# Seven-product units in the feed-forward blocks of a decoder trunk: four a block instead of three, two low parts a block on GpSimd, another order of VectorE's sums

## The chip, the cores and the metric

The kernel runs on one core of a Trainium2 chip. The metric is the device time of one execution in microseconds (us). Engines are called by their names in the profile: PE is TensorE, DVE is VectorE, ACT is ScalarE, POOL is GpSimd, SP is SyncE, whose queue issues the loads of the weights.

## The reference, cut to what matters

The program is one layer of a hybrid decoder with 256 tokens, 2048 model columns and a feed-forward width of 5632. The change touches only its last part:

```
u = rmsnorm(h, pre_ffn_g)                                     # 256 x 2048
ff = (silu(u @ w_gate) * (u @ w_up)) @ w_down                 # 2048 -> 5632 -> 2048
h = h + rmsnorm(ff, post_ffn_g)
```

All inputs are float32.

## The kernel before

**Precision.** A float32 operand is split into a high part (rounded to the fp32r format of PE) and a low part (the rest). A product is then three matmuls into one PSUM bank: high by high, high by low, low by high (`three`, L1705). ACT makes the high parts of the weights (`split_hi`, L557, line L561 in the profile), DVE the low parts as `raw - w_hi` (`split_lo`, L908, line L910).

**Stages.** After the mixing layers (up to 346 us) come eleven feed-forward blocks, g = 0 to 10 (`NFG`). A block makes 512 columns of gate and 512 of up. Its 16 chunks q = BEGIN[g] + ch (ch = 0 to 15) each hold 128 rows of w_gate and w_up side by side, 128x1024 float32, 512 KB, loaded with two DMAs (line L447). Two blocks of w_down with 44 chunks each follow (g = 11 and 12). Everything goes through a ring of four slots (`WSLOTS`): `raw` (loaded), `w_hi`, `w_lo`. Chunk q + 4 takes the slot of chunk q.

**Plain chunks and seven-product units.** A plain chunk is four quarters (two halves of the tokens, gate and up) of three matmuls each: 12 matmuls of 128x512. Two successive chunks can also form a *unit of seven products* (Strassen-Winograd): 7 products instead of 8, so 21 matmuls instead of 24. `ROUND` says by a letter for each pair of chunks whether it is plain (P) or a unit (Z); before, blocks 1 to 10 have `PPZPZPZP`, that is units at ch 4-5, 8-9 and 12-13. A unit needs sums of the weights, which DVE makes in `weight_sums` (L1186): sum 0 (L1197, 128x512), the low half of the first chunk (L1183), sum 1 (L1202), and sums 2 and 3 in one instruction (L1206, 128x1024). Then comes the low part of the second chunk (L910), and after ACT's high parts of the sums (L841, two of 128x1024), their low parts (`weight_sums_lo`, L1213, two of 128x1024). Sum 0 waits for the raw data of both chunks. The sums stand in one buffer, `tx`. A unit also needs sums of the token rows (`input_sums`, made once for each pair of row tiles in `SEVEN_F`, in block 0).

**The end of a block.** When PE has done a block's last unit, ACT copies one PSUM bank to `tx` (`x0_kept`, L891), in its program behind the high part of ch 1 of the next block, and DVE makes `fold_sums` (L1267, L1271, L1274), in its program behind the low part of ch 1. When PE has done the whole block, DVE adds them to the quarters (`fold`, L1280 twice, and `fold_up`, L1284), ACT takes the silu (L818), DVE multiplies (`gated`, L1171 twice): this is `inner_product`, at ch 3 of the next block. PE then transposes the result (`turn_inner`, L1769) ahead of ch 2, for which it waits for `p_done`, the end of the second L1171. ACT and DVE split the transposed tiles (`inner_hi`, L822; `inner_lo`, L1176, semaphore `f_lo`), at ch 5 (`INNER_AT`).

**Banks.** PE transposes into two banks that the products m7 and m6 of the block's units use. So in the block's first unit PE waits ahead of m6 for `inner_lo`:

```
three(m5, row_sum(0), weight_sum(0), begin, end).then_inc(t_used, 1)
if begin and g <= NFG:
    pe.wait_ge(f_lo, g)
three(m6, row_sum(1), weight_sum(1), begin, end).then_inc(t_used, 1)
```

**Order and slots.** Each engine runs its program in the order of q, as written out in the loops over q; nothing is reordered. SP issues the loads in the order of q. For the load of chunk q it waits until chunk q - 4 has its low part (`lo_done`), and, if q - 4 is in a unit, until that unit's sums 2 and 3 are made:

```
if (before, d_b) in SEVEN_NO:
    sp_eng.wait_ge(t_made, 3 * SEVEN_NO[before, d_b] + 3)
```

ACT makes the high part of chunk q once it is loaded and PE has used chunk q - 4 (`chunks_used`). POOL's program ends before the feed-forward blocks begin.

Of the kernel before, what the change touches and what calls it, by code (L numbers as in the profile page):

```python
# [24 lines left out]
P = 128  # L25
# [11 lines left out]
def build_trunk(nc, x, meta, pre_mix_g, w_in, w_pool, pool_scale, w_dw, b_dw, conv_ln_g, conv_ln_b, w_pw,  # L37
# [93 lines left out]
    ROUND = ["PPPPPPPP"] + ["PPZPZPZP"] * (NFG - 1) + ["PPPPZPPZPPZPPZPZPZPZPP", "PPPZPZPZPZPZPZPZPZPZPP"]  # L131
    BEGIN = [Q_FFN + KT * g for g in range(NFG)] + [Q_DOWN + FT * n for n in range(DW)]
# [12 lines left out]
    QUARTERS = [(0, 0), (0, 1), (1, 0), (1, 1)]  # L145
    INNER_AT = 5
    FOLDS_F = len(QUARTERS) * (NFG - 1)
    assert DW == 2 and ROUND[NG - 1].endswith("P" * (LAST // 2)) and all(d in SUM_NO for d in SEVEN_U)

    def place_of(q):  # L150
        g = max(g for g in range(NG) if BEGIN[g] <= q)
        ch = q - BEGIN[g]
        return g, ch, TURNS[g][ch // 2]

    def landed(q):
# [5 lines left out]
    with ExitStack() as ctx:  # L161
# [37 lines left out]
        sums_f = sb_at("sums_f", [P, len(SEVEN_F), 4, 2, P], F32R, a_y)  # L199
        gated = sb_at("gated", [P, NQ, DCOLS], F32, a_y + 4 * KT * SEQ - 8 * DCOLS)  # L200
        sums_y = sb_at("sums_y", [P, max(len(SEVEN_U) - IN_U, 1), 3, 2, P], F32R, a_y)
        assert 32 * P * len(SEVEN_F) + 8 * DCOLS <= 4 * KT * SEQ and 24 * P * (len(SEVEN_U) - IN_U) <= 4 * KT * SEQ
# [108 lines left out]
        def sem(name):  # L311
            return ctx.enter_context(nc.semaphore(name))
# [87 lines left out]
        def _(sp_eng):  # L400
# [64 lines left out]
        def _(pool):  # L465
# [90 lines left out]
        def _(act):  # L556
# [350 lines left out]
        def _(dve):  # L907
# [278 lines left out]
            def weight_sums(q, z):  # L1186

                at = [(q - 1) % WSLOTS, q % WSLOTS]
                b11, b12, b22 = (raw[:, at[k], j * DCOLS:(j + 1) * DCOLS] for k, j in ((0, 0), (0, 1), (1, 1)))
                for k in range(2):  # L1190
                    dve.wait_ge(raw_landed[at[k]], landed(q - 1 + k))
                if z == 0:
                    dve.wait_ge(s_lo, 2 * len(SEVEN_F))
                else:
                    dve.wait_ge(t_used, 4 * z - 3)
                    dve.wait_ge(fold_done, len(QUARTERS) * max(min(SEVENS[z][0], NFG) - 1, 0))
                dve.tensor_tensor(tx[:, 0, :], b12, b11, ALU.add).then_inc(t_made, 1)  # L1197
# [169 lines left out]
        def _(pe):  # L1367
# [346 lines left out]
            def right(q, j):  # L1714
                at = slice(j * DCOLS, (j + 1) * DCOLS)
                return [w_hi[:, q % WSLOTS, at], w_lo[:, q % WSLOTS, at]]

            def plain_products(q, quarters):
                g, ch, d = place_of(q)
                kt, chs = 2 * d + ch % 2, 2 * len(ROUND[g])  # L1720
                pe.wait_ge(lo_done, q + 1)
                if g >= NFG:
                    pe.wait_ge(f_lo, kt // 4 + 1)
                for m, j in quarters:
                    if g == 0:
                        pe.wait_ge(h2_lo, CK * m + kt + 1 if kt < CK else CK + kt + 1)
                    mm = three(quarter(g, m, j), left(g, kt, m), right(q, j), ch == 0, ch == chs - 1)
                return mm

            def seven_products(q):  # L1730
# [110 lines left out]
```

## Time and profile before

| | |
|---|---|
| median of 3 runs | 1076.29 us (1075.73 to 1076.4) |
| the profiled execution, its own time | 1075.67 us |
| its span in the profile | 1073.7 us |
| PE busy | 1063.8 us (99%), 5731 matmuls |
| DVE busy | 891.5 us (83%) |
| ACT busy | 598.3 us (56%) |
| POOL busy | 31.5 us (3%) |
| granted clock of PE | 0.999 of full speed |
| DMA, mean | 194 GB/s |

The own time is the span and some 2 us around it. In the rows below a time is in us from the start of the span. In a timeline a row is: start, duration, engine, line, operation, output and inputs, shape, how many were merged, and in brackets the idle time before it with what ended it. Instructions of one engine overlap a little: the next one starts before the one ahead of it ends. So what an instruction occupies on its engine is the distance from its start to the next start, not its duration.

### The profile page before, as it was taken

Reading aid. Unit: us, or ns where it says so; the run is one execution under the profiler, and the core shown is the slowest. Engines: PE = TensorE matmul, PEld = TensorE weight load, DVE = VectorE, ACT = ScalarE, POOL = GpSimd, SP = SyncE. Lnnn points to the kernel's source line nnn. Section 1 sums busy time; section 2 is a strip of 40 time slices with the busy share of each in tenths; the row PEclk is TensorE's granted clock in tenths of the full one; section 3 lists DMA queues with packets and bytes.
Section 4 is the critical chain, followed back from the end, with each engine's and each line's share of the span. In section 5 each row is a group of like instructions: output and inputs, shape, how many; then the busy total and the mean of one; then the engine's idle time right before and its main releaser. Section 6 shows DMA issues by size and latency. Waiting matters only on the chain. (4 is left out here: it accounts for less than half of the span.)

```text
span 1073.7 us, 15358 instructions
## 1 busy us (share of the span) xinstructions
PE 1063.8 (99%) x5731; PEld 921.6 (86%) x5731; DVE 891.5 (83%) x1082; ACT 598.3 (56%) x735; POOL 31.5 (3%) x49
## 2 busy tenths in 40 slices
PE   9999999999999999999999999999999999999997
PEld 8999999999888888888888888888888888888885
DVE  6699987646646787898998998988989899988887
ACT  6554454736545565555565655655655555655553
POOL 6000001101000000000000000000000000000000
PEclk9999999999999999999999999999999999999999
DMA  8655535444386475756756656657656666566665
GB/s 271 216 176 166 172 105 162 135 143 135 112 309 214 140 266 185 225 188 193 223 174 195 216 180 212 195 181 231 189 185 222 223 200 197 189 208 214 208 200 196
DMA packets 113208, 208.06 MB, mean 194 GB/s; under 512 B 9184, under 2 KB 46496, under 8 KB 111856
## 3 DMA queue, kind: packets, MB, share of 16 engines
q1 hardware_dynamic: 111952, 201.49, 58.8%
q10 hardware_dynamic: 608, 4.20, 1.0%
q0 software_dynamic: 576, 1.40, 0.4%
q8 instruction: 46, 0.75, 0.3%
q14 instruction: 26, 0.21, 0.1%
HBM read 202.86 MB, written 4.19 MB: 193 GB/s over the span
## 5 line engine op out<-in xcount | busy, mean ns | idle before, releaser
L561 ACT ACTIVATE w_hi<-raw 128x1024 fp32r<-128x1024 f32 x321 | 337.1, 1059 | 259.0 <-PE ps L1708 153.0
L910 DVE TENSOR_TENSOR w_lo<-raw,w_hi 128x1024 fp32r<-128x1024 f32 x321 | 389.6, 1226 | 84.0 <-ACT w_hi L561 83.4
L1706 PE MATMUL ps<-w_hi,uf 128*128 128x512 f32 x524 | 205.3, 392 | 0.1
L1708 PE MATMUL ps<-w_hi,uf 128*128 128x512 f32 x524 | 204.1, 389 | 0.0
L1707 PE MATMUL ps<-w_lo,uf 128*128 128x512 f32 x524 | 203.9, 389 | 0.0
L1377 PE MATMUL ps<-u,w_hi 128*128 128x272 f32 (+1 forms) x544 | 158.8, 292 | 0.0
L1379 PE MATMUL ps<-u,w_hi 128*128 128x272 f32 (+1 forms) x544 | 155.9, 287 | 0.0
L1380 PE MATMUL ps<-u,w_lo 128*128 128x272 f32 (+1 forms) x544 | 155.7, 286 | 0.0
L841 ACT CAST t_hi<-tx 128x1024 fp32r<-128x1024 f32 x92 | 96.4, 1053 | 67.7 <-DVE tx L1202 56.4
L1708 PEld LDWEIGHTS ps<-w_hi,uf 128*128 128x128 f32 x524 | 98.4, 188 | 20.6
L1706 PEld LDWEIGHTS ps<-w_hi,uf 128*128 128x128 f32 x524 | 98.4, 188 | 20.5 <-issue 0.5
L1707 PEld LDWEIGHTS ps<-w_lo,uf 128*128 128x128 f32 x524 | 98.4, 188 | 20.0
L1213 DVE TENSOR_TENSOR t_lo<-tx,t_hi 128x1024 fp32r<-128x1024 f32 x92 | 108.2, 1218 | 0.0
L1377 PEld LDWEIGHTS ps<-u,w_hi 128*128 128x128 f32 x544 | 102.4, 188 | 0.4
L1379 PEld LDWEIGHTS ps<-u,w_hi 128*128 128x128 f32 x544 | 102.5, 188 | 0.2
L1380 PEld LDWEIGHTS ps<-u,w_lo 128*128 128x128 f32 x544 | 102.5, 188 | 0.0
L1706 PE MATMUL ps<-w_hi,ffn 128*128 128x512 f32 x256 | 99.7, 389 | 0.0
L1708 PE MATMUL ps<-w_hi,ffn 128*128 128x512 f32 x256 | 99.6, 389 | 0.0
L1707 PE MATMUL ps<-w_lo,ffn 128*128 128x512 f32 x256 | 99.6, 389 | 0.0
L1206 DVE TENSOR_TENSOR tx<-raw,tx 128x1024 f32<-128x1024 f32 x46 | 56.4, 1226 | 4.7
L1707 PEld LDWEIGHTS ps<-w_lo,ffn 128*128 128x128 f32 x256 | 48.1, 188 | 10.0
L1708 PEld LDWEIGHTS ps<-w_hi,ffn 128*128 128x128 f32 x256 | 48.1, 188 | 9.9
(277 smaller groups left out, 1473.2 us busy)
## 6 DMA issues: line engine op xcount, KB each, us to landing
raw<-in_w_gate SPq DMA_DIRECT2D x176, 256.0 KB, 3.0
raw<-in_w_up SPq DMA_DIRECT2D x176, 256.0 KB, 3.5
raw<-in_w_down SPq DMA_DIRECT2D x88, 512.0 KB, 4.2
raw<-in_w_in SPq DMA_DIRECT2D x72, 512.0 KB, 3.6
raw<-in_w_out SPq DMA_DIRECT2D x32, 512.0 KB, 4.7
arena<-in_x SPq DMA_DIRECT2D x2, 1024.0 KB, 6.2
arena<-in_x ACTq DMA_DIRECT2D x2, 1024.0 KB, 8.7
out<-h2rows SPq DMA_DIRECT2D x2, 1024.0 KB, 5.5
```

The source lines that it names most:

```text
L561: act.activation(w_hi[:, slot, :], raw[:, slot, :], ACT.Copy).then_inc(hi_done, 1)
L841: act.copy(t_hi[:, 2 * h:2 * h + 2, :], tx[:, 2 * h:2 * h + 2, :]).then_inc(t_hi_done, 1)
L910: dve.tensor_tensor(w_lo[:, slot, :], raw[:, slot, :], hi_view(w_hi[:, slot, :]), ALU.subtract).then_inc(lo_done, 1)
L1206: dve.tensor_tensor(tx[:, 2:4, :], raw[:, at[0]:at[0] + 2, 0:DCOLS], tx[:, 1:2, :].to_broadcast([P, 2, DCOLS]), ALU.add).then_inc(t_made, 1)
L1213: dve.tensor_tensor(t_lo[:, 2 * h:2 * h + 2, :], tx[:, 2 * h:2 * h + 2, :], hi_view(t_hi[:, 2 * h:2 * h + 2, :]), ALU.subtract).then_inc(t ...
L1377: pe.matmul(outs[m], w_hi[:, slot, at], x_hi, start=start and not (one_bank and m), stop=False, skip_group_check=True)
L1379: pe.matmul(outs[m], w_hi[:, slot, at], x_lo, start=False, stop=False, skip_group_check=True)
L1380: mm = pe.matmul(outs[m], w_lo[:, slot, at], x_hi, start=False, stop=last and k == len(kts) - 1, skip_group_check=True)
L1706: pe.matmul(o, a[0], b[0], start=start, stop=False)
L1707: pe.matmul(o, a[0], b[1], start=False, stop=False)
L1708: return pe.matmul(o, a[1], b[0], start=False, stop=stop)
```

## The change

It does four things. Blocks 1 to 7 (`WITH_SPARE`) get a fourth unit: `PZPZPZZP`, units at ch 2-3, 6-7, 10-11 and 12-13; blocks 8 to 10 keep their order. In those blocks `inner_hi` and `inner_lo` stand at ch 4, and the first unit's sums (ch 3) stand in DVE's program ahead of `inner_product`, its low parts behind it; ACT makes the high parts of that unit's sums ahead of the high part of ch 3. POOL makes two of DVE's low parts a block: of ch 3 of blocks 1 to 7 (`IN_PRODUCT`, after the first `fold`) and of ch 1 of blocks 2 to 8 (`IN_FOLD`, after ACT's copy of x0); PE and SP wait for these on a semaphore of their own, `lo_pool`. The sums get a second buffer (`tx2`, `t_hi2`, `t_lo2`), which the units of blocks 1 to 7 use in turn. And in every unit, those of the later blocks too, the low part of the second chunk (`split(q)`) moves up between sum 1 and sums 2 and 3. Block 0 makes the row sums of a fourth pair.

```diff
-    SEVEN_F, SEVEN_U = (0, 1, 2), (11, 12, 13, 14, 15, 16, 17, 18, 19)
+    SEVEN_F, SEVEN_U = (0, 1, 2, 3), (11, 12, 13, 14, 15, 16, 17, 18, 19)
-    F_SUM_AT = {10: 0, 12: 1, 14: 2}
-    ROUND = ["PPPPPPPP"] + ["PPZPZPZP"] * (NFG - 1) + [...]
+    F_SUM_AT = {10: 0, 12: 1, 13: 2, 14: 3}
+    WITH_SPARE = range(1, 8)
+    ROUND = ["PPPPPPPP"] + ["PZPZPZZP" if g in WITH_SPARE else "PPZPZPZP" for g in range(1, NFG)] + [...]
-    INNER_AT = 5
+    INNER_AT = [4 if g in WITH_SPARE else 5 for g in range(NFG + 1)]
+    IN_PRODUCT = {BEGIN[g] + 3: g for g in WITH_SPARE}
+    IN_FOLD = {BEGIN[g + 1] + 1: g for g in WITH_SPARE}
+    BY_POOL = sorted([*IN_PRODUCT, *IN_FOLD])
...
+    def buffers_of(z):
+        g, d = SEVENS[z]
+        return (z - SEVENS_TO[g - 1] + 1) % 2 if g in WITH_SPARE else 0
...
@@ SP
-                sp_eng.wait_ge(lo_done, q - WSLOTS + 1)
+                if q - WSLOTS in POOL_NO:
+                    sp_eng.wait_ge(lo_pool, POOL_NO[q - WSLOTS] + 1)
+                else:
+                    sp_eng.wait_ge(lo_done, lo_by_dve(q - WSLOTS))
@@ POOL
+            for q in BY_POOL:
+                slot = q % WSLOTS
+                if q in IN_FOLD:
+                    pool.wait_ge(x0_kept, IN_FOLD[q])
+                elif IN_PRODUCT[q] > 1:
+                    pool.wait_ge(fold_done, len(QUARTERS) * (IN_PRODUCT[q] - 2) + 1)
+                pool.wait_ge(hi_done, q + 1)
+                pool.tensor_tensor(w_lo[:, slot, :], raw[:, slot, :], w_hi[:, slot, :].bitcast(F32),
+                                   ALU.subtract).then_inc(lo_pool, 1)
@@ ACT
                     if z is not None and ch % 2 == 0:
                         first_half_hi(q)
+                    elif q in IN_PRODUCT:
+                        weight_sums_hi(z)
+                        split(q)
                     else:
                         split(q)
@@ DVE, weight_sums
                 dve.tensor_tensor(sums[:, 1, :], b22, sums[:, 0, :], ALU.subtract).then_inc(t_made, 1)
+                if q not in POOL_NO:
+                    split(q)
...
                 dve.tensor_tensor(sums[:, 2:4, :], ...).then_inc(t_made, 1)
@@ DVE, loop over q
+                    if q in IN_PRODUCT:
+                        weight_sums(q, z)
                     if 1 <= g <= NFG and ch == 3:
                         dve.wait_ge(chunks_used, BEGIN[g])
                         inner_product(g - 1)
-                    if z is None:
+                    if z is None and q not in POOL_NO:
                         split(q)
-                    elif ch % 2:
+                    elif q in IN_PRODUCT:
+                        weight_sums_lo(z)
+                    elif z is not None and ch % 2:
                         weight_sums(q, z)
-                        split(q)
                         weight_sums_lo(z)
-                    if 1 <= g <= NFG and ch == INNER_AT:
+                    if 1 <= g <= NFG and ch == INNER_AT[g]:
                         inner_lo(g - 1)
```

## Rows read from the trace of the kernel before

**Rows 1.** The page: busy time, share of the span and instructions of each engine.
```profile
PE 1063.8 (99%) x5731; PEld 921.6 (86%) x5731; DVE 891.5 (83%) x1082; ACT 598.3 (56%) x735; POOL 31.5 (3%) x49
```
**Rows 2.** Busy time of each engine in one block (stretch; length, then engines; clock, DMA).
```profile
454.70:497.10 42.40, 42.40 (x193) 35.18 (x192) 38.59 (x40) 24.11 (x27) 0.00 (x0) 1.00 0.64 198
```
**Rows 3.** Timeline of PE: chunks 0 and 1 of block 3, transposes, chunk 2.
```profile
497.06 0.39 PE L1707 MATMUL ps<-w_lo,uf 128*128 128x512 f32 x1
...
502.04 0.39 PE L1708 MATMUL ps<-w_hi,uf 128*128 128x512 f32 x1
502.28 1.03 PE L1769 MATMUL ps<-cst,gated 128*128 128x128 f32 x8
503.07 0.48 PE L1706 MATMUL ps<-w_hi,uf 128*128 128x512 f32 x1
```
**Rows 4.** Timeline of DVE: a unit (ch 12-13 of block 2) and its low parts.
```profile
479.52 0.69 DVE L1197 TENSOR_TENSOR tx<-raw 128x512 f32<-128x512 f32 x1 [0.51 <-PE ps L1708]
480.12 0.68 DVE L1183 TENSOR_TENSOR w_lo<-raw,w_hi 128x512 fp32r<-128x512 f32 x1
480.73 0.68 DVE L1202 TENSOR_TENSOR tx<-raw,tx 128x512 f32<-128x512 f32 x1
481.51 1.23 DVE L1206 TENSOR_TENSOR tx<-raw,tx 128x1024 f32<-128x1024 f32 x1
482.66 1.22 DVE L910 TENSOR_TENSOR w_lo<-raw,w_hi 128x1024 fp32r<-128x1024 f32 x1
483.79 2.35 DVE L1213 TENSOR_TENSOR t_lo<-tx,t_hi 128x1024 fp32r<-128x1024 f32 x2
486.06 1.22 DVE L910 TENSOR_TENSOR w_lo<-raw,w_hi 128x1024 fp32r<-128x1024 f32 x1
```
**Rows 5.** Timeline of DVE: fold sums and inner product between blocks 2 and 3.
```profile
492.28 0.69 DVE L1267 TENSOR_TENSOR tx<-ps,tx 128x512 f32<-128x512 f32 x1 [0.80 <-ACT tx L891]
...
494.33 0.69 DVE L1274 TENSOR_TENSOR tx<-ps,tx 128x512 f32<-128x512 f32 x1
...
497.13 1.30 DVE L1280 TENSOR_TENSOR ps<-ps,tx 128x512 f32<-128x512 f32 x2 [0.44 <-PE ps L1708]
...
499.76 1.41 DVE L1171 SCALAR_TENSOR_TENSOR gated<-ps,cst,gated 128x512 f32<-128x512 f32 x2 [0.20 <-DVE ps L1284]
501.08 1.22 DVE L910 TENSOR_TENSOR w_lo<-raw,w_hi 128x1024 fp32r<-128x1024 f32 x1
```
**Rows 6.** Timeline of ACT: copy of x0 for that fold.
```profile
491.59 0.59 ACT L891 COPY tx<-ps 128x512 f32<-128x512 f32 x1 [1.60 <-PE ps L1708]
```
**Rows 7.** Timelines of POOL, DVE in the mixing stage: POOL alone, then both at once.
```profile
189.87 1.27 POOL L533 TENSOR_TENSOR side<-side 128x512 f32<-128x512 f32 x1 [21.52 <-ACT side L726]
...
248.62 1.99 POOL L533 TENSOR_TENSOR side<-side 128x512 f32<-128x512 f32 x1 [55.80 <-ACT side L741]
...
249.51 2.18 DVE L910 TENSOR_TENSOR w_lo<-raw,w_hi 128x1024 fp32r<-128x1024 f32 x1
251.62 0.47 DVE L975 SCALAR_TENSOR_TENSOR ffn<-ps,cst,ffn 128x256 fp32r<-128x256 f32 x1
...
250.69 1.60 POOL L535 TENSOR_TENSOR side<-side 128x256 f32<-128x256 f32 x1
```
**Rows 8.** Timelines of DVE, SP, ACT: sums made, four DMAs, wait for them.
```profile
504.21 1.23 DVE L1206 TENSOR_TENSOR tx<-raw,tx 128x1024 f32<-128x1024 f32 x1
...
506.97 0.43 SPq L447 DMA_DIRECT2D raw<-in_w_up  x1
...
511.23 1.06 ACT L561 ACTIVATE w_hi<-raw 128x1024 fp32r<-128x1024 f32 x1 [0.80 <-DMA raw<-in_w_up]
```
**Rows 9.** Timeline of ACT at the start of block 1: high part, table load, silu.
```profile
412.31 1.06 ACT L561 ACTIVATE w_hi<-raw 128x1024 fp32r<-128x1024 f32 x1 [1.66 <-PE ps L1708]
413.39 1.28 ACT L818 ACT_TABLE_LOAD   x1
414.68 1.27 ACT L818 ACTIVATE gated<-ps,cst 128x512 f32<-128x512 f32 x2
```

More of the change, by code:

```diff
@@ L126, in build_trunk @@
     NG = NFG + DW
-    SEVEN_F, SEVEN_U = (0, 1, 2), (11, 12, 13, 14, 15, 16, 17, 18, 19)
+    SEVEN_F, SEVEN_U = (0, 1, 2, 3), (11, 12, 13, 14, 15, 16, 17, 18, 19)
     SUM_AT = {4: 11, 10: 12, 12: 13, 18: 14, 22: 15, 24: 16, 28: 17, 32: 18, 36: 19}
     SUM_NO = {d: i for i, d in enumerate(SUM_AT.values())}
-    F_SUM_AT = {10: 0, 12: 1, 14: 2}
-    ROUND = ["PPPPPPPP"] + ["PPZPZPZP"] * (NFG - 1) + ["PPPPZPPZPPZPPZPZPZPZPP", "PPPZPZPZPZPZPZPZPZPZPP"]
+    F_SUM_AT = {10: 0, 12: 1, 13: 2, 14: 3}
+    WITH_SPARE = range(1, 8)
+    ROUND = ["PPPPPPPP"] + ["PZPZPZZP" if g in WITH_SPARE else "PPZPZPZP" for g in range(1, NFG)] + ["PPPPZPPZPPZPPZPZPZPZPP", "PPPZPZPZPZPZPZPZPZPZPP"]
     BEGIN = [Q_FFN + KT * g for g in range(NFG)] + [Q_DOWN + FT * n for n in range(DW)]
@@ L153, in place_of, with lo_by_dve, before_in_buffers @@
         return g, ch, TURNS[g][ch // 2]
+    IN_PRODUCT = {BEGIN[g] + 3: g for g in WITH_SPARE}
+    IN_FOLD = {BEGIN[g + 1] + 1: g for g in WITH_SPARE}
+    BY_POOL = sorted([*IN_PRODUCT, *IN_FOLD])
+    POOL_NO = {q: i for i, q in enumerate(BY_POOL)}
+    def lo_by_dve(q):
+        return q + 1 - sum(1 for a in BY_POOL if a <= q)
+    def buffers_of(z):
+        g, d = SEVENS[z]
+        return (z - SEVENS_TO[g - 1] + 1) % 2 if g in WITH_SPARE else 0
+    def before_in_buffers(z):
+        return max((y for y in range(z) if buffers_of(y) == buffers_of(z)), default=None)
     def landed(q):
@@ L192, in build_trunk @@
         t_hi = sb_at("t_hi", [P, 4, DCOLS], F32R, a_xt + 16 * DCOLS)
+        a_spare = top[0] + 4 * KT * SEQ + 4 * 1152 + 4 * 4 * (max(WITH_SPARE) + 1) * 2 * SEQ
+        tx2 = sb_at("tx2", [P, 4, DCOLS], F32, a_spare)
+        t_lo2 = sb_at("t_lo2", [P, 4, DCOLS], F32R, a_spare)
+        t_hi2 = sb_at("t_hi2", [P, 4, DCOLS], F32R, a_spare + 16 * DCOLS)
+        sums_of, hi_of, lo_of = (tx, tx2), (t_hi, t_hi2), (t_lo, t_lo2)
         rows_u = tx[:, 0, :].rearrange("p (k t) -> p k t", k=2)
@@ L199, in build_trunk @@
         sums_f = sb_at("sums_f", [P, len(SEVEN_F), 4, 2, P], F32R, a_y)
-        gated = sb_at("gated", [P, NQ, DCOLS], F32, a_y + 4 * KT * SEQ - 8 * DCOLS)
+        gated = sb_at("gated", [P, NQ, DCOLS], F32, a_spare + 32 * DCOLS)
         sums_y = sb_at("sums_y", [P, max(len(SEVEN_U) - IN_U, 1), 3, 2, P], F32R, a_y)
-        assert 32 * P * len(SEVEN_F) + 8 * DCOLS <= 4 * KT * SEQ and 24 * P * (len(SEVEN_U) - IN_U) <= 4 * KT * SEQ
+        assert 32 * P * len(SEVEN_F) <= 4 * KT * SEQ and 24 * P * (len(SEVEN_U) - IN_U) <= 4 * KT * SEQ
         side = sb_at("side", [P, KT * SEQ], F32, a_y)
@@ L207, in build_trunk @@
         a_ff = place(4 * FT * 2 * SEQ)
+        assert a_spare == a_ff + 4 * 32 * 2 * SEQ and 32 * DCOLS + 8 * DCOLS <= 4 * 12 * 2 * SEQ
         ffn = sb_at("ffn", [P, FT, 2, SEQ], F32R, a_ff)
@@ L1191, in weight_sums @@
                     dve.wait_ge(raw_landed[at[k]], landed(q - 1 + k))
-                if z == 0:
+                sums, y = sums_of[buffers_of(z)], before_in_buffers(z)
+                if z <= 1:
                     dve.wait_ge(s_lo, 2 * len(SEVEN_F))
-                else:
-                    dve.wait_ge(t_used, 4 * z - 3)
+                if y is not None:
+                    dve.wait_ge(t_used, 4 * y + 1)
+                if y is not None and buffers_of(z) == 0:
                     dve.wait_ge(fold_done, len(QUARTERS) * max(min(SEVENS[z][0], NFG) - 1, 0))
-                dve.tensor_tensor(tx[:, 0, :], b12, b11, ALU.add).then_inc(t_made, 1)
+                dve.tensor_tensor(sums[:, 0, :], b12, b11, ALU.add).then_inc(t_made, 1)
                 first_half_lo(q - 1)
-                if z:
-                    dve.wait_ge(t_used, 4 * z - 2)
+                if y is not None:
+                    dve.wait_ge(t_used, 4 * y + 2)
                 dve.wait_ge(t_made, 3 * z + 1)
-                dve.tensor_tensor(tx[:, 1, :], b22, tx[:, 0, :], ALU.subtract).then_inc(t_made, 1)
-                if z:
-                    dve.wait_ge(t_used, 4 * z)
+                dve.tensor_tensor(sums[:, 1, :], b22, sums[:, 0, :], ALU.subtract).then_inc(t_made, 1)
+                if q not in POOL_NO:
+                    split(q)
+                if y is not None:
+                    dve.wait_ge(t_used, 4 * y + 4)
                 dve.wait_ge(t_made, 3 * z + 2)
-                dve.tensor_tensor(tx[:, 2:4, :], raw[:, at[0]:at[0] + 2, 0:DCOLS],
-                                  tx[:, 1:2, :].to_broadcast([P, 2, DCOLS]), ALU.add).then_inc(t_made, 1)
+                dve.tensor_tensor(sums[:, 2:4, :], raw[:, at[0]:at[0] + 2, 0:DCOLS],
+                                  sums[:, 1:2, :].to_broadcast([P, 2, DCOLS]), ALU.add).then_inc(t_made, 1)
             def weight_sums_lo(z):
+                b = buffers_of(z)
                 dve.wait_ge(t_made, 3 * z + 3)
@@ L1212, in weight_sums_lo @@
                     dve.wait_ge(t_hi_done, 2 * z + h + 1)
-                    dve.tensor_tensor(t_lo[:, 2 * h:2 * h + 2, :], tx[:, 2 * h:2 * h + 2, :],
-                                      hi_view(t_hi[:, 2 * h:2 * h + 2, :]), ALU.subtract).then_inc(t_lo_done, 1)
+                    dve.tensor_tensor(lo_of[b][:, 2 * h:2 * h + 2, :], sums_of[b][:, 2 * h:2 * h + 2, :],
+                                      hi_view(hi_of[b][:, 2 * h:2 * h + 2, :]), ALU.subtract).then_inc(t_lo_done, 1)
             def four_sums(i, hi, lo, r, s):
@@ L1303, in _ @@
                         inner_product(g - 1)
-                    if z is None:
+                    if z is None and q not in POOL_NO:
                         split(q)
-                    elif ch % 2:
+                    elif q in IN_PRODUCT:
+                        weight_sums_lo(z)
+                    elif z is not None and ch % 2:
                         weight_sums(q, z)
-                        split(q)
                         weight_sums_lo(z)
-                    if 1 <= g <= NFG and ch == INNER_AT:
+                    if 1 <= g <= NFG and ch == INNER_AT[g]:
                         inner_lo(g - 1)
@@ L1716, in right, with weights_split @@
                 return [w_hi[:, q % WSLOTS, at], w_lo[:, q % WSLOTS, at]]
+            def weights_split(q):
+                if q in POOL_NO:
+                    pe.wait_ge(lo_pool, POOL_NO[q] + 1)
+                else:
+                    pe.wait_ge(lo_done, lo_by_dve(q))
             def plain_products(q, quarters):
@@ L1720, in plain_products @@
                 kt, chs = 2 * d + ch % 2, 2 * len(ROUND[g])
-                pe.wait_ge(lo_done, q + 1)
+                weights_split(q)
                 if g >= NFG:
@@ L1740, in weight_sum @@
                 def weight_sum(t):
-                    return [t_hi[:, t, :], t_lo[:, t, :]]
-                pe.wait_ge(lo_done, q + 1)
+                    return [hi_of[buffers_of(z)][:, t, :], lo_of[buffers_of(z)][:, t, :]]
+                weights_split(q)
                 if g < NFG:
```

6 lines of the change are left out of this document (4 added, 2 removed).

## The prediction

> **What bounds the kernel now.** The page's first part: PE is busy for 1063.8 us, 99% of the span [rows 1]. The busy time by stretches says how that is inside a block: a feed-forward block of three units takes 42.40 us, in which PE never rests and DVE is busy for 38.59 us, ACT for 24.11 [rows 2]. So fewer matmuls shorten the kernel, if their operands come in time. PE's timeline gives prices: 22 matmuls from 497.06 to 502.04, 0.226 us each; transposes to next chunk 0.8 us [rows 3].
>
> **T** below is the moment at which PE is done with a block; DVE's fold, which waited for it, started at 497.13, so T = 497.1 [rows 5]. PE started its transposes at T + 5.2 and chunk 2 at T + 6.0 [rows 3]: it needs `p_done` by T + 5.2.
>
> **The gain.** Seven units more, one in each of blocks 1 to 7, save three matmuls each: 21 x 0.226 = 4.8 us. A block would take 42.4 - 0.7 = 41.7 us. If nothing else moved, that would be the result. I think it does not get there, for two reasons.
>
> **Prices on DVE**, as distances between starts [rows 4]: a 128x512 sum or half low part 0.60; a low part, or sums 2 and 3, 1.14; `t_lo` of a unit 2.27 (483.79 to 486.06). Sums 2 and 3 right behind sum 1 start 0.78 after it, as they wait for its result. `fold_sums` takes 2.66 (492.28 to 494.33 and 0.61), `inner_product` 3.95 (497.13 to 501.08) [rows 5]. A unit with its second low part takes 3 x 0.60 + 2 x 1.14 + 2.27 = 6.4; its sums 2 and 3 are made 4.2 after its first sum starts (0.6 + 0.6 + 0.6 + 1.14 + 1.23), where they were before it 3.2: the move of the low part fills a gap of 0.1 us and makes the sums 1 us later, and SP's loads into the unit's two slots wait for the sums.
>
> DVE's work in a block of four units: three units 19.2; the first unit, whose second low part is POOL's, 0.6 + 0.6 + 0.78 + 1.14 = 3.1 for the sums and 2.27 for `t_lo`; seven of the eight plain chunks' low parts 8.0; `fold_sums`, `inner_product`, `inner_lo` 2.66 + 3.95 + 1.14. Together 40.3 of the 41.7 us. DVE can afford 1.4 us of waits a block; now it has 42.4 - 38.6 = 3.8 [rows 2].
>
> **A low part on POOL.** POOL alone took 1.27 us for 512 elements [rows 7], and 0.6 for 256 (the 1.60 of its row, 250.69 to 252.29, less the 1.0 in which DVE's operation, until 251.69, still held it up). Stretched to 1024 that is 2.4 (four times 0.6) to 2.6 (1.27 and two steps of 0.67); I take 2.4, as each of the short ones has its start in it, and 0.14 until it starts, an estimate. The rows also show who stands still: POOL's 1.99 ends at 250.61, DVE's low part, both inputs in SBUF, started at 249.51 and took 2.18 in place of 1.22, to 1.08 after POOL's end; but DVE's L975, which reads PSUM and one SBUF tensor, took 0.47 in the middle of a POOL operation [rows 7]. So POOL's low part of ch 1 is free beside `fold_sums`, and that of ch 3 beside the folds, but not beside `t_lo`.
> By the Trainium skill ("GPSIMD Engine Reference", Performance versus the Vector engine) GpSimd's add of 2048 float32 elements takes 4497 ns, so an estimate of 2.25 us for 1024. With it the loop below would be 0.15 us shorter and the result some 1 us lower; no run yet shows that size.
>
> **First reason: the bank of m6.** ACT copies x0 at T - 5.5 [rows 6], once PE is done with the last unit; DVE starts `fold_sums` at T - 4.8 [rows 5]. It is done at T - 2.2, and the new first unit's sums 3.1 later. Call **W** the moment at which DVE is free of them: W = T + 1.0 at the earliest. From there: `inner_product` 4.05 (ACT's silu now stands behind two high parts, of the sums and of ch 3, and is just in time: W + 0.1 + 2 x 1.0, first silu to W + 2.7, gated after it), so `p_done` at W + 4.15 = T + 5.15, met by a hair. POOL's low part of ch 3 starts when its high part is made, W + 2.15 + 0.14, and ends at W + 4.7: DVE's first `t_lo` waits 0.6 for it. Then 2.27, low part of ch 4 1.14, `inner_lo` 1.22: W + 9.3 = T + 10.3. PE, though, now has its first unit at ch 2: it starts at T + 6.0, and after 12 matmuls, at T + 8.7, waits for `inner_lo` to give back the bank of m6. It stands still 1.6 us, 1.0 even if POOL holds nobody up. Before, the first unit was at ch 4, 5.4 us later. So even with DVE on time the block takes 41.7 + 1.0 to 1.6, **more than the 42.4 of before**.
>
> **Second reason: DVE's loop through the loads.** After sums 2 and 3 of a unit (end 505.44) SP issues two chunks, and ACT starts on the second at 511.23: 5.8 us [rows 8]. The next unit's sum 0 waits for both. In the new order:
> 1. W to sums 2, 3 of unit 2 (ch 6-7): 4.05 + 0.6 + 2.27 + 1.14 + 1.14 + 1.14 + 4.2 = 14.5.
> 2. Unit 3 (ch 10-11) takes unit 2's slots: 5.8 + 4.2 = 10.0. DVE has only `t_lo` and two low parts in between (4.5), so it waits 1.3.
> 3. Unit 4 (ch 12-13) right after: 2.2 + 4.2 = 6.4.
> 4. Ch 0 and 1 of the next block take unit 4's slots: 5.8 to ch 1's data, 1.06 for its high part [rows 8], 0.6 for x0 behind it [rows 6]: 7.5 to `fold_sums`. DVE waits 1.8.
> 5. `fold_sums` and the next first sums: 2.66 + 3.14 = 5.8.
> Sum 44.2 us from W to W, where PE would need 41.7. So DVE falls behind, and from block 3 on every block takes 44.2: PE waits for `p_done` and `inner_lo`.
> The same steps for the order of before (three units four chunks apart, two low parts in between) give under 40: there PE leads, as the trace shows.
>
> **The sum.** Block 1: DVE's program in block 0 is 2.3 us longer (the fourth row sums), hidden from PE. T is 412.3, when ACT could begin the high part of ch 3, and I estimate W = 413.6, much as in the later blocks. ACT's high parts of sums 2 and 3 and of ch 3 come ahead of its one table load (1.28) and the silu (1.27) [rows 9]: 415.7, 417.0, 418.3, and the second gated ends at 419.1, where PE wants it at 417.5: 1.6 lost; the bank costs 0.9 more. T of block 2 is 454.7 - 0.7 + 2.5 = 456.5. Its W, by steps 2 to 5, is 458.5; five loops on, W of block 7 is 458.5 + 5 x 44.2 = 679.5; and PE from W: chunk 2 at W + 5.0, 14 chunks of 156 matmuls 35.7 with the gap at their start, bank 1.6, gives W + 42.3 = 721.8 for the end of block 7. Before it is 497.1 + 5 x 42.4 = 709.1. Loss **12.7**. Blocks 8 to 10 and w_down have the old order: DVE catches up in block 8 behind `fold_sums`, and the low part moved there costs nothing, since DVE waits for PE in every unit there (0.5 before sum 0 [rows 4]); without that cover it would be 1 us a unit. The last stretch is unchanged. The profiled execution's 1075.7 (span 1073.7 and 2.0 around it), 0.6 under the median, would become 1088.4; the median 1076.3 becomes **1089.0**.
> Bounds: if the loop is 43.4 (data 0.4 sooner each time, POOL in nobody's way) the loss is 8.7; if it is 45.0 (POOL's 2.6, loads 0.3 later) 16.7.
>
> **Rivals.**
> *A, the loads do not bind* (they land sooner, or DVE is ahead): then only the bank holds PE, 0.3 to 0.9 a block more than before, six times, and 1.8 in block 1: 4 to 7 us, 1076.3 + 5.4 = 1081.7. For: DVE's work alone fits (40.3). Against: 5.8 us for the second load. 15%.
> *B, faster*: `inner_lo` is done before PE gets to m6, and the loads do not bind. It decides at T + 8.7: `inner_lo` would have to be done 1.6 us sooner than I find. Then the saved 21 matmuls count in full: 1076.3 - 4.8 = 1071.5. Against: the four steps on DVE ahead of it, all priced. 10%.
> *C, POOL stops all of DVE*, PSUM operations too: 2.4 more in `fold_sums` and 1 in `inner_product`, six times: 20 us more, 1109. Against: L975's 0.47 beside POOL [rows 7]. The Trainium skill ("SBUF — State Buffer", Who interferes with whom) also has DVE instructions with one SBUF input free of GpSimd; by it the sum stays. 4%.
> *D, gain and wait cancel*: the bank alone, and a wait of only 0.7 a block: 1076.3. 4%.
>
> **Chances.** Main case 67%, its own range 1085 to 1093 by the bounds. The range of 8 in 10 takes in most of A: 1079 to 1093. A measurement of this kernel can tell some 0.2% (2 us) from no change. Faster by over 0.2%: 0.10 (B); within: 0.05 (D, the edge of A); slower: 0.85.
>
> **What would show it.** Right: PE idle in each of blocks 2 to 7, some 1.6 us ahead of the first L1706 of m6, released by DVE's L1176, and some ahead of L1769, released by L1171; DVE idle 1.3 before sum 0 of unit 3 (released by a load) and 1.8 before L1267; blocks of 44.2 us; POOL's 14 low parts at 2.4 to 2.6; `t_lo` once a block at 1.8 in place of 1.22. Wrong: PE without gaps and blocks of 41.7 (B); gaps only at m6 and blocks of 43 (A); L1267 and L1271 longer beside POOL (C).

## The result, and the profile after

| | before | after |
|---|---|---|
| median of the runs | 1076.01 us (4 runs, 1075.68 to 1076.4) | 1090.95 us (4 runs, 1089.71 to 1091.37) |
| ratio, 95% interval | | 1.0137 (1.0124 to 1.0149) |
| span in the profile | 1073.7 us | 1089.5 us |

The change makes the kernel 1.4% slower; predicted were 1089.0 us, in a range of 1079 to 1093. The first part of the page after answers to [rows 1]:

```profile
PE 1061.8 (97%) x5710; PEld 914.7 (84%) x5710; DVE 908.5 (83%) x1109; ACT 605.7 (56%) x750; POOL 65.1 (6%) x63
```

PE has the 21 matmuls less that were forecast (5731 to 5710), POOL 14 instructions more. PE is no longer busy all the time (97% of the span in place of 99%). The list of waits of the profile after, 400 to 745 us (who waited for whom: us in total, times, longest):

```profile
ACT w_hi L599 <- DMA raw<-in_w_up: 27.9, 28, 2.8
...
DVE tx L1314 <- ACT tx L933: 12.3, 7, 3.2
...
PE ps L1825 <- DVE gated L1213: 8.3, 7, 1.8
PE ps L1756 <- DVE ffn L1218: 7.5, 7, 1.2
```

The last two are the waits of the prediction: seven ahead of the transposes (L1825, released by `gated`) and seven ahead of m6 (L1756, released by `inner_lo`). Before there was none of either. L1314 is the first instruction of `fold_sums`, which waits for x0. Its starts give the length of the blocks, and this is how blocks are measured in all that follows: the distance from the first to the seventh of these instructions, by six. After:

```profile
453.65 0.69 DVE L1314 TENSOR_TENSOR tx<-ps,tx 128x512 f32<-128x512 f32 x1 [1.17 <-ACT tx L933]
...
676.40 0.69 DVE L1314 TENSOR_TENSOR tx<-ps,tx 128x512 f32<-128x512 f32 x1 [1.46 <-ACT tx L933]
```

The seventh stands at 720.38: (720.38 - 453.65) / 6 = 44.5 us, where before it was (704.21 - 449.87) / 6 = 42.4. Behind the seventh start the distances are 42.2, 41.8 and 42.4, about those of before. DVE's timeline of the kernel after, where block 3 begins (the counterpart of [rows 5]):

```profile
497.95 0.69 DVE L1314 TENSOR_TENSOR tx<-ps,tx 128x512 f32<-128x512 f32 x1 [1.68 <-ACT tx L933]
498.74 1.23 DVE L1318 TENSOR_TENSOR tx<-ps,tx 128x1024 f32<-128x1024 f32 x1
500.00 0.69 DVE L1321 TENSOR_TENSOR tx<-ps,tx 128x512 f32<-128x512 f32 x1
500.82 0.70 DVE L1241 TENSOR_TENSOR tx<-raw 128x512 f32<-128x512 f32 x1
...
502.82 1.23 DVE L1252 TENSOR_TENSOR tx<-raw,tx 128x1024 f32<-128x1024 f32 x1
503.96 1.29 DVE L1327 TENSOR_TENSOR ps<-ps,tx 128x512 f32<-128x512 f32 x2
...
508.02 2.80 DVE L1260 TENSOR_TENSOR t_lo<-tx,t_hi 128x1024 fp32r<-128x1024 f32 x2
...
511.88 1.21 DVE L1218 TENSOR_TENSOR ffn<-ps,ffn 128x1024 fp32r<-128x1024 f32 x1
```

POOL's timeline in the same stretch:

```profile
497.92 2.41 POOL L582 TENSOR_TENSOR w_lo<-raw,w_hi 128x1024 fp32r<-128x1024 f32 x1 [33.83 <-ACT tx L933]
506.24 2.37 POOL L582 TENSOR_TENSOR w_lo<-raw,w_hi 128x1024 fp32r<-128x1024 f32 x1 [5.91 <-ACT w_hi L599]
```

And PE's, the counterpart of [rows 3]:

```profile
508.16 1.09 PE L1825 MATMUL ps<-cst,gated 128*128 128x128 f32 x8 [1.15 <-DVE gated L1213]
...
511.63 0.39 PE L1758 MATMUL ps<-t_hi,sums_f 128*128 128x512 f32 x1
513.15 0.50 PE L1756 MATMUL ps<-t_hi,sums_f 128*128 128x512 f32 x1 [1.13 <-DVE ffn L1218]
513.48 0.40 PE L1757 MATMUL ps<-t_lo,sums_f 128*128 128x512 f32 x1
```

In these three the reader sees: POOL's first low part (497.92 to 500.33) lies beside `fold_sums`, which takes what it took before; its second (506.24 to 508.61) meets `t_lo`, whose pair takes 2.80 in place of 2.35. `inner_lo` ends at 513.09, and PE, which could have gone on at 511.9, starts m6 at 513.15.

### The profile page after: what moved, and what is told of

Read it like the earlier page. It is cut to its first block and busy times, and to the rows that moved or that the text cites. A ratio compares the mean times of both kernels' runs of the same rounds, so it can differ in the third digit from the quotient of the medians.

```text
span 1089.5 us, 15429 instructions
## 1 busy us (share of the span) xinstructions
PE 1061.8 (97%) x5710; PEld 914.7 (84%) x5710; DVE 908.5 (83%) x1109; ACT 605.7 (56%) x750; POOL 65.1 (6%) x63
## 5 line engine op out<-in xcount | busy, mean ns | idle before, releaser
L599 ACT ACTIVATE w_hi<-raw 128x1024 fp32r<-128x1024 f32 x314 | 328.3, 1058 | 199.6 <-PE ps L1758 65.1
L952 DVE TENSOR_TENSOR w_lo<-raw,w_hi 128x1024 fp32r<-128x1024 f32 x300 | 364.6, 1226 | 77.6 <-ACT w_hi L599 76.8
L1756 PE MATMUL ps<-w_hi,uf 128*128 128x512 f32 x482 | 189.0, 392 | 0.5 <-DVE tx L1321 0.4
L1758 PE MATMUL ps<-w_hi,uf 128*128 128x512 f32 x482 | 187.7, 389 | 0.0
L1757 PE MATMUL ps<-w_lo,uf 128*128 128x512 f32 x482 | 187.6, 389 | 0.0
L880 ACT CAST t_hi<-tx 128x1024 fp32r<-128x1024 f32 x106 | 111.7, 1053 | 130.9 <-DVE tx L1246 71.8
L1260 DVE TENSOR_TENSOR t_lo<-tx,t_hi 128x1024 fp32r<-128x1024 f32 x106 | 127.7, 1246 | 1.6
L1756 PEld LDWEIGHTS ps<-w_hi,uf 128*128 128x128 f32 x482 | 90.5, 188 | 19.7 <-DVE tx L1321 0.8
L1758 PEld LDWEIGHTS ps<-w_hi,uf 128*128 128x128 f32 x482 | 90.5, 188 | 18.9
L1757 PEld LDWEIGHTS ps<-w_lo,uf 128*128 128x128 f32 x482 | 90.5, 188 | 18.3
L1756 PE MATMUL ps<-w_hi,ffn 128*128 128x512 f32 x256 | 99.7, 389 | 0.0
L1252 DVE TENSOR_TENSOR tx<-raw,tx 128x1024 f32<-128x1024 f32 x53 | 64.5, 1218 | 0.7
L582 POOL TENSOR_TENSOR w_lo<-raw,w_hi 128x1024 fp32r<-128x1024 f32 x14 | 33.5, 2392 | 436.5 <-ACT tx L933 238.7
L1756 PEld LDWEIGHTS ps<-w_hi,ffn 128*128 128x128 f32 x256 | 48.0, 188 | 10.0
## 6 DMA issues: line engine op xcount, KB each, us to landing
arena<-in_x ACTq DMA_DIRECT2D x2, 1024.0 KB, 10.2
```

The source lines that it names most:

```text
L582: pool.tensor_tensor(w_lo[:, slot, :], raw[:, slot, :], w_hi[:, slot, :].bitcast(F32), ALU.subtract).then_inc(lo_pool, 1)
L599: act.activation(w_hi[:, slot, :], raw[:, slot, :], ACT.Copy).then_inc(hi_done, 1)
L880: act.copy(hi_of[b][:, 2 * h:2 * h + 2, :], sums_of[b][:, 2 * h:2 * h + 2, :]).then_inc(t_hi_done, 1)
L952: dve.tensor_tensor(w_lo[:, slot, :], raw[:, slot, :], hi_view(w_hi[:, slot, :]), ALU.subtract).then_inc(lo_done, 1)
L1252: dve.tensor_tensor(sums[:, 2:4, :], raw[:, at[0]:at[0] + 2, 0:DCOLS], sums[:, 1:2, :].to_broadcast([P, 2, DCOLS]), ALU.add).then_inc(t_ma ...
L1260: dve.tensor_tensor(lo_of[b][:, 2 * h:2 * h + 2, :], sums_of[b][:, 2 * h:2 * h + 2, :], hi_view(hi_of[b][:, 2 * h:2 * h + 2, :]), ALU.subt ...
```

## The experiments

Theory L: two things hold PE. The first is a loop, DVE's work and the loads that wait for a unit's sums; it sets the length of a block. The second is the bank of m6, which would set it if the loop were shorter. Against L stand a theory that counts the bank alone (K), and smaller ones named with each run. A result outside the range that was expected is called a miss. "Blocks" is the measure above; the kernel before has 42.4, the kernel after 44.5. Times are medians beside the kernel before on the same chip (1076.1 in the first four, 1075.7 to 1075.8 in the others).

**e1_order_alone.** Kernel before, with one move:
```diff
                 dve.tensor_tensor(tx[:, 1, :], b22, tx[:, 0, :], ALU.subtract).then_inc(t_made, 1)
+                split(q)
...
                         weight_sums(q, z)
-                        split(q)
                         weight_sums_lo(z)
```


> The kernel before, with only the new place of a unit's second low part (between sum 1 and sums 2 and 3), in all units. Theory L (after the change it is DVE's loop through the loads that sets the length of a block): three units stand four chunks apart, so the sums 1 us later stay hidden behind PE's lead; time as before, 1075 to 1077, TensorE without gaps. Rival M (the moved low part is costly by itself, in every unit and in w_down too): 46 units at up to 1 us, 1080 or more.

Measured: 1076.39 us, ratio 1.0002 (0.9992 to 1.0012). No difference that these runs can tell, and PE waits for nothing from 400 to 745 us. The move costs nothing where PE leads.

**e2_low_part_back.** Kernel after, the same move undone in every unit.
```diff
-                if q not in POOL_NO:
-                    split(q)
...
                                   sums[:, 1:2, :].to_broadcast([P, 2, DCOLS]), ALU.add).then_inc(t_made, 1)
+                if q not in POOL_NO:
+                    split(q)
```


> The kernel after, with the second low part back behind sums 2 and 3 in every unit; the rest stays. Theory L: the sums of units 2 and 3 are ready 1 us sooner each, so the loop shrinks from the measured 44.4 us to about 42.5, less than TensorE needs with its wait for the bank (41.7 + 1.6 = 43.3): blocks of 43.3, 1083 us (1081 to 1086), the waits for L1213 (turning) mostly gone, those for L1218 (bank of m6) as they are. Rival K (only the bank counts, and the wait ahead of the transposes follows from it): no change, 1090.

Measured: 1084.25 us, ratio 1.0077 (1.0061 to 1.0094); blocks 43.3. 6.7 us of the 15 come from a move that cost nothing in e1. The waits of this kernel, 400 to 745 us:
```profile
PE ps L1756 <- DVE ffn L1218: 7.7, 7, 1.2
...
PE ps L1825 <- DVE gated L1213: 1.8, 1, 1.8
```
Ahead of the transposes only block 1's wait is left; the bank is as before. So the block is now what PE needs with its wait for the bank. ACT says the same: its copy of x0, which in the kernel after starts right behind the high part of ch 1 in all seven blocks, now waits for PE:
```profile
579.97 1.06 ACT L599 ACTIVATE w_hi<-raw 128x1024 fp32r<-128x1024 f32 x1 [1.15 <-DMA raw<-in_w_up]
581.48 0.59 ACT L933 COPY tx<-ps 128x512 f32<-128x512 f32 x1 [0.45 <-PE ps L1758]
```
Rival K, which wanted 1090, falls.

**e3_x0_first.** Kernel after, ACT's x0 ahead of the high part of ch 1 (and no longer behind it).
```diff
+                    if q in IN_FOLD:
+                        act.wait_ge(t_used, 4 * SEVENS_TO[g - 1])
+                        act.copy(tx[:, 0, :], sevens_bank(g - 1, 0)).then_inc(x0_kept, 1)
                     if z is not None and ch % 2 == 0:
                         first_half_hi(q)
```


> The kernel after, with ACT's copy of x0 ahead of the high part of ch 1 in place of behind it (blocks 2 to 8), so that the fold sums no longer wait for a load. Theory L: the loop shrinks by the 1.7 us and more that DVE waits there (measured 1.2 to 3.2), to 42.5 or so; TensorE's wait for the bank then sets the block: 43.3, 1083 us (1081 to 1086). Rival K: no change, 1090.

Measured: 1089.29 us, ratio 1.0122 (1.0105 to 1.0139); blocks 44.3. A miss: 1083 was expected. DVE's timeline of this run shows why:
```profile
540.95 0.69 DVE L1317 TENSOR_TENSOR tx<-ps,tx 128x512 f32<-128x512 f32 x1 [0.86 <-ACT tx L905]
541.74 1.23 DVE L1321 TENSOR_TENSOR tx<-ps,tx 128x1024 f32<-128x1024 f32 x1
543.00 0.69 DVE L1324 TENSOR_TENSOR tx<-ps,tx 128x512 f32<-128x512 f32 x1
544.62 1.03 DVE L1244 TENSOR_TENSOR tx<-raw 128x512 f32<-128x512 f32 x1 [0.92 <-DMA raw<-in_w_up]
```
The fold sums wait less (0.86 where the kernel after waits 3.21 in that block, its longest; 3.9 in place of 12.3 us in all), but right behind them sum 0 waits 0.92 for a load, and then runs 1.03 beside POOL. Behind the wait that was taken away lay another (the load), and behind that POOL's hold. The theory becomes L2: once unit 4's sums are made, the loads of chunks 0 to 3 follow each other, and the last sets when the next unit's sum 0 can start.

**e4_bank_late.** Kernel after, the bank freed in time: `inner_hi`, `inner_lo` at the end of ch 3, and in a block's first unit
```diff
+                if begin and g in WITH_SPARE:
+                    pe.wait_ge(t_lo_done, 2 * z + 2)
+                    three(quarter(g, 1, 0), left(g, 2 * d + 1, 1), weight_sum(3)).then_inc(t_used, 1)
                 if begin and g <= NFG:
                     pe.wait_ge(f_lo, g)
```
(the units of these blocks then wait for all four products of the unit whose buffer they take).

> The kernel after, with the wait for the bank of m6 taken away: in blocks 1 to 7 DVE's inner_lo and ACT's inner_hi stand at the end of ch 3, ahead of the low and high part of ch 4, and TensorE does the product for quarter (1,0) of a block's first unit ahead of m6. Theory L: the seven waits for L1218 (8.6 us in all) go, but the wait ahead of the transposes grows by as much, since DVE's loop keeps its 44.4 us: 1088 to 1091. Rival K: the 8.6 us are won, 1082.

Measured: 1089.2 us, ratio 1.0126 (1.0109 to 1.0143); blocks 44.2. Its waits, 400 to 745 us:
```profile
PE ps L1832 <- DVE gated L1213: 10.3, 7, 1.7
PE ps L1756 <- DVE tx L1321: 3.2, 6, 0.9
```
The seven waits for the bank (7.5 us) are gone. The wait ahead of the transposes has grown from 8.3 to 10.3, and the one in the second row from 0.4 to 3.2: PE, early in a block, waits for the last of the fold sums (L1321). Of the 7.5 us, 4.8 came back in these two, and the time fell by 1.8. With the loop in place, the bank was nearly free. DVE has a new wait in this run, 8.1 us ahead of sum 0 (8 times, put down to nothing that the profile shows). The last load of a pair landed 0.08 us before each of these starts (in block 3 it was issued at 519.50 and landed 4.2 us later, and sum 0 of unit 3 starts at 523.77), so it is the loads that DVE waits for, and not the four products.

**e5_loads_lighter.** e3, with fewer bytes in the row of loads: of the up half of chunks 2 and 3 only 64 of 512 columns are loaded, so part of the up projection is left out.
```diff
+                        n = 64 if j and ch in (2, 3) and g in IN_FOLD.values() else DCOLS
-                        sp_eng.dma_start(raw[:, q % WSLOTS, j * DCOLS:(j + 1) * DCOLS],
+                        sp_eng.dma_start(raw[:, q % WSLOTS, j * DCOLS:j * DCOLS + n],
```


> The kernel of e3_x0_first, in which the fold sums came sooner but sum 0 of a block's first unit then waited 0.8 to 0.9 us for loads. Here the up half of chunks 2 and 3 of blocks 1 to 7 is loaded for 64 of its 512 columns (the rest of it is what the slot held, so that this part of the up projection is left out); everything else is issued as before. Theory L2 (four chunks are loaded in a row once unit 4's sums are made, and their bytes set when sum 0 can start): 0.45 MB less in the row of four makes it land some 1.8 us sooner, the wait of L1244 for a load goes, blocks shrink by 0.8 us or more toward the 43.3 that TensorE needs with its bank: 1084 (1082 to 1086). Rival N (the wait has to do with the place in the program or in the queue, not with bytes): 1089 as e3.

Measured: 1086.96 us, ratio 1.0105 (1.0088 to 1.0122); blocks 43.8. The same place in DVE's timeline:
```profile
541.49 0.69 DVE L1325 TENSOR_TENSOR tx<-ps,tx 128x512 f32<-128x512 f32 x1
542.10 1.29 DVE L1245 TENSOR_TENSOR tx<-raw 128x512 f32<-128x512 f32 x1
```
The wait for the load is gone with the bytes, so L2 holds and rival N falls. But the time is 1 us above the range, a miss. More than half of what the 0.9 us could bring is lost at once: sum 0, started sooner, meets POOL's low part (540.44 to 542.85) and takes 1.29 in place of 0.69.

**e6_no_pool.** Kernel after, `BY_POOL` empty, ch 3's low part ahead of `t_lo` on DVE.

> The kernel after, with VectorE making the two low parts again (that of ch 3 ahead of the first unit's low parts, that of ch 1 ahead of the fold sums). Theory L: ch 1's part falls into VectorE's wait ahead of the fold sums and costs nothing; ch 3's costs its 1.14 us less the 0.45 that GpSimd held t_lo up (2.80 in place of 2.35): blocks 0.7 us longer, 1095 (1093 to 1098). Rival P (GpSimd holds VectorE up by as much as it takes off it): 1090 or less.

Measured: 1105.92 us, ratio 1.0276 (1.0256 to 1.0296); blocks 46.5. A miss by 11 us, and rival P is further off. DVE at the turn from one block to the next:
```profile
547.78 1.23 DVE L952 TENSOR_TENSOR w_lo<-raw,w_hi 128x1024 fp32r<-128x1024 f32 x1 [2.03 <-ACT w_hi L599]
548.93 0.68 DVE L1314 TENSOR_TENSOR tx<-ps,tx 128x512 f32<-128x512 f32 x1
```
The expectation put ch 1's low part into DVE's wait ahead of the fold sums. But it has to wait for the same high part as x0, and stands behind that wait: 1.15 in place of x0's 0.65. That and ch 3's 0.7 make 1.2 of the 2.0 us a block. The rest lies between the sums of unit 2 and those of unit 4 (17.5 us on the mean of the six blocks, in place of 16.5). In four of the six blocks DVE waits there ahead of ch 9's low part for ACT, and ACT for PE:
```profile
575.14 1.23 DVE L952 TENSOR_TENSOR w_lo<-raw,w_hi 128x1024 fp32r<-128x1024 f32 x1 [1.49 <-ACT w_hi L599]
```
```profile
574.05 1.06 ACT L599 ACTIVATE w_hi<-raw 128x1024 fp32r<-128x1024 f32 x1 [1.66 <-PE ps L1759]
```
So a late PE can hold the loop up in turn; what makes it late there was not tried. POOL's two low parts are worth 15 us against DVE making them at these places: they are the good half of the change.

**e7_bank_and_low_part** is e2 and e4 together.

> e2 and e4 together: second low part back behind the sums, and the bank of m6 freed in time. Each alone left the other limit. Theory L: the loop is then 13.4 + 9.0 + 6.5 + 7.5 + 5.8 = 42.2 us, TensorE's own need 41.7: blocks of 42.2, and block 1's wait for its silu stays (2.0 less 0.7): 1076 to 1079. Rival Q (the low part and the bank act on the same wait, so that together they bring no more than the better one): 1084.

Measured: 1079.98 us, ratio 1.0039 (1.0025 to 1.0054), 1 us above the range, a miss. e2 alone won 6.7 us and e4 alone 1.8, together they win 11.0: two limits one behind the other, so rival Q falls. (The profiled execution took 1083.34, so its blocks, 43.2, are longer than the median's.)

**e8_all_four** is e7 with e3, and with POOL's start in ch 3 brought forward:
```diff
                     elif q in IN_PRODUCT:
-                        weight_sums_hi(z)
+                        weight_sums_hi(z, [0])
                         split(q)
+                        weight_sums_hi(z, [1])
```


> e7_bank_and_low_part with x0 copied ahead of ch 1's high part, and ACT's high part of ch 3 between the two halves of the unit's high sums, so that GpSimd's part of ch 3 starts 1 us sooner and is done when t_lo begins. Theory L: the loop falls under TensorE's 41.7 us or just to it, the transposes are met by a hair: blocks of 41.7 to 42, 1073.5 (1072 to 1077). Rival L2 (the row of four loads keeps the loop where it is): as e7_bank_and_low_part.

Measured: 1077.44 us, the median of ten runs, one of which took 5216.82; without that one it is 1077.09, and the ratio 1.0012 (1.0002 to 1.0022) is taken from the nine. Blocks 42.6. Just above the range, a miss, though 3 us better than e7, which rival L2 had put it level with. DVE's timeline:
```profile
582.63 0.69 DVE L1245 TENSOR_TENSOR tx<-raw 128x512 f32<-128x512 f32 x1 [0.91 <-DMA raw<-in_w_up]
...
589.72 2.35 DVE L1264 TENSOR_TENSOR t_lo<-tx,t_hi 128x1024 fp32r<-128x1024 f32 x2
```
`t_lo` is back at 2.35, as meant. Sum 0 waits 0.91 for the row of loads.

**e9_own_chunk.** e8; sum 0 reads only the unit's first chunk, so it waits for that one alone.
```diff
-                for k in range(2):
-                    dve.wait_ge(raw_landed[at[k]], landed(q - 1 + k))
+                dve.wait_ge(raw_landed[at[0]], landed(q - 1))
...
+                dve.wait_ge(raw_landed[at[1]], landed(q))
                 dve.wait_ge(t_made, 3 * z + 1)
```


> e8_all_four, and a unit's sum 0 waits for its first chunk's data alone (it reads no other); the wait for the second chunk's data stands ahead of sum 1, 1.2 us later, in all units. Theory L2: what is left in e8 is VectorE's wait of 0.9 us for chunk 3's load behind the fold sums, which comes out as TensorE's 0.7 us ahead of the transposes in six blocks; it goes, blocks come to 41.8: 1073.5 (1072.5 to 1075), under the kernel before. Rival R (the 0.7 us come from ACT's chain up to the silu): no change, 1077.

Measured: 1075.55 us, ratio 0.9998 (0.9989 to 1.0007); blocks 42.3. A miss, half of what was expected: 1.5 to 1.9 us less than e8 (by which of its medians is taken), where 3.9 were expected. PE's wait ahead of the transposes in six blocks fell from 0.4 to 1.1 us to 0.34 in each, but not to nothing, for the reason of e5 (sum 0 takes 1.29). Rival R, which wanted no change, falls.

**e10_from_block_2** is e9 with `WITH_SPARE = range(2, 8)`: block 1 has three units again.

> e9_own_chunk with four units only in blocks 2 to 7: block 1, where the first unit's high sums stand ahead of ACT's table load and the silu, goes back to three units. It lost 1.7 us ahead of the transposes there and won 0.7: 1 us less than e9_own_chunk, 1072.5 (1071.5 to 1074). If the wait in block 1 has to do with block 0's fourth row sums in place of the order in block 1, no gain.

Measured: 1074.48 us, ratio 0.9986 (0.9977 to 0.9995): 1.1 us less than e9, the step that was expected (the time itself is 0.5 above the range, as e9 was). Each of blocks 3 to 7 still has this on DVE and on PE:
```profile
495.16 1.29 DVE L1244 TENSOR_TENSOR tx<-raw 128x512 f32<-128x512 f32 x1
```
```profile
502.99 1.09 PE L1836 MATMUL ps<-cst,gated 128*128 128x128 f32 x8 [0.34 <-DVE gated L1217]
```

**e11_spread_units** is e10 with `PZPZZPZP`.

> e10_from_block_2 with the units at ch 2-3, 6-7, 8-9 and 12-13 in place of 2-3, 6-7, 10-11 and 12-13: the third and fourth unit no longer stand together, so that the loads they let go come more evenly. Theory L2: no shorter, since the row of four loads still starts with unit 4's sums, whose place in VectorE's work is the same: within 1 us of e10_from_block_2. Rival S (two units in a row are what makes the end of a block late): 1 to 3 us less.

Measured: 1074.75 us, ratio 0.9991 (0.9982 to 1.0). No difference that the runs can tell from e10, so rival S falls: whether the third unit stands at ch 8-9 or at ch 10-11 does not matter here.

**e12_x0_behind** is e10 without e3's move.

> e10_from_block_2 with ACT's copy of x0 back behind the high part of ch 1. In e10 TensorE still waits 0.5 us ahead of the transposes in five blocks, and VectorE's sum 0 there takes 1.29 us in place of 0.69, for GpSimd's low part of ch 1 (493.50 to 495.91) starts 1 us later than it could, its high part being made behind x0. Theory G (GpSimd's hold on sum 0 is that half microsecond): with the high part first, GpSimd is done before sum 0, which falls back to 0.69; the fold sums stay, since the load of ch 1 lands just in time; the 0.5 us go: 1072.0 (1071.3 to 1073.3). Rival L (the load of ch 1, now ahead of x0 again, makes the fold sums late, as in the kernel after): no gain or a loss, 1074.5 to 1077.

Measured: 1073.73 us (11 runs, 1071.91 to 1074.82), ratio 0.9977 (0.9968 to 0.9986), **0.2% faster than the kernel before**. It lies between the ranges of theory G and rival L. DVE at the start of block 3:
```profile
494.35 0.68 DVE L1241 TENSOR_TENSOR tx<-raw 128x512 f32<-128x512 f32 x1
```
Both views were right in part. Sum 0 is back at 0.68, and in the blocks where ch 1's load lands in time PE has no wait at all (501.61 for the transposes, right behind the last matmul). In three of five it does not, ACT's high part of ch 1 waits for it, x0 and the fold sums come late, and PE waits up to 0.9. ACT's timeline at such a place, ahead of block 5:
```profile
575.59 1.06 ACT L599 ACTIVATE w_hi<-raw 128x1024 fp32r<-128x1024 f32 x1 [1.17 <-DMA raw<-in_w_up]
576.56 0.56 ACT L934 COPY tx<-ps 128x512 f32<-128x512 f32 x1
```
The three waits make 1.8 us, most of the 2.8 that this execution (1074.82) is over the 1072.0 of the expectation; the median is 1.7 over it.

## Why the prediction was right

**The gain.** 21 matmuls fewer, as counted.

**The bank of m6.** Predicted: a stand of 1.6 us a block, 1.0 without POOL's hold. Measured: the wait is 1.13 us, and from 511.63 to 513.48 two distances take 1.85 in place of 0.45, so the stand costs 1.4. The order of events was as worked out; the term is 0.2 too large, as `t_lo` was held up 0.45 and not 0.6. e4 shows what the text had not said: with the loop in place, this wait costs almost nothing of its own.

**The loop.** Predicted 44.2 us from W to W, measured 44.5 on the mean. The five steps, in the kernel after, over the six blocks that begin with the fold sums from 453.65 to 676.40:

| step | predicted, us | measured mean (least to most) |
|---|---|---|
| 1, W to the sums of unit 2 | 14.5 | 14.3 (14.3 to 14.4) |
| 2, to the sums of unit 3 | 10.0 | 9.7 (9.1 to 10.2) |
| 3, to the sums of unit 4 | 6.4 | 6.7 (6.5 to 7.3) |
| 4, to the fold sums | 7.5 | 7.8 (7.3 to 9.0) |
| 5, to the next W | 5.8 | 5.9 (5.8 to 6.1) |

The path is the one that was forecast; that the total is so close is partly luck, since steps 1 and 2 were too long and steps 3 and 4 too short by 0.2 to 0.3 each. Step 2 had DVE wait 1.3 ahead of sum 0 of unit 3; it waits 0 to 1.0, 0.5 on the mean. Step 4 varies most: it took 7.5 into block 3 (490.47 to 497.95) but 9.0 into block 4, where ACT has
```profile
542.05 1.06 ACT L599 ACTIVATE w_hi<-raw 128x1024 fp32r<-128x1024 f32 x1 [2.83 <-DMA raw<-in_w_up]
```
7.4 us after the sums' end at 534.67, in place of 5.8. e3 and e5 add that step 4 was a limit with another just behind it, the row of loads to chunk 3, which the prediction did not have.

**The moved low part.** Predicted: 1 us in step 1 and step 2 each, nothing where PE leads. e1 (no change) shows the second. For the first, e2 wins 6.7 us: step 1 falls from 14.3 to 13.4 and step 2 from 9.7 to 9.2, with PE holding the block at step 4.

**POOL.** Predicted 2.4 us for a low part, measured 2.37 to 2.41 in all 14. The estimate of 2.25, half of what the Trainium skill gives for 2048 elements ("GPSIMD Engine Reference", Performance versus the Vector engine), is 6% under it. POOL holds up DVE instructions with both inputs in SBUF, and none of those that read PSUM; this is seen again: `t_lo` 2.80 and sum 0 1.29 (e5), fold sums and gated unchanged. Rival C falls. The Trainium skill ("SBUF — State Buffer", Who interferes with whom) says that a DVE instruction with two SBUF inputs contends with a GpSimd instruction that reads SBUF, and one with at most one SBUF input does not; the trace agrees.

**Block 1.** Predicted 1.6 and 0.9 of waiting, measured 1.82 and 0.69. In e9, where the wait for the bank is gone, giving the block its three units back (e10) brings 1.1 us. The fourth row sums in block 0 cost PE nothing, as forecast: the transposes of block 1 start at 417.49 in e12, which still makes these sums, and at 417.50 before.

**The rivals.** A (loads do not bind) is refuted by e2 and e5, B by the waits, D by the time.

**The sum.** It was 2 us too small: 12.7 against 14.9. In the profiled execution W of block 2 stands at 459.4 where the sum had 458.5, and the five loops from there to W of block 7 (682.2) take 44.55 us each in place of 44.2, 1.7 more.

## What to carry to other kernels

How busy an engine is (DVE had 38.6 of 42.4 us a block [rows 2]) does not decide whether more work fits on it; what decides is when its instructions release the buffer slots, for every load behind them starts there. So before work is added to a block, follow the chain from one block's start to the next through the queue of loads, and compare its length with the bound engine's. A wait that is removed shows the next one: here the low part, the bank, the row of loads, GpSimd's hold and chunk 1's load stood one behind the other, and only several edits together turned a loss of 15 us into a gain of 2. That is half of the 4.1 us that e12's 18 matmuls less (5713) are worth at 0.226 us each.

## What was not expected of the hardware

A pair of loads released by a unit's sums landed 5.8 us later in one block and 7.4 in the next, in one execution; which loads share the queues at that moment was not tried by itself. Moving one DVE instruction to the shadow of POOL's was enough to double it (0.69 to 1.29, e5 and e10), and POOL's instruction did not get longer for it (2.41 with and without). The held instruction ended 0.54 us after POOL's (e5: 543.39 and 542.85), a little less than the 0.69 that it takes alone.
